# Layer norm of a two-layer decoder trunk: moments summed while tiles are finished, statistics with tokens on partitions, two units prepared for the next stage

## The reference

```python
def layernorm(x, g, b):
    xf = x.astype(F32)
    mu = jnp.mean(xf, -1, keepdims=True)
    var = jnp.mean(jnp.square(xf - mu), -1, keepdims=True)
    return ((xf - mu) * lax.rsqrt(var + LN_EPS) * g + b).astype(x.dtype)

for layer in range(DEPTH):
    ...
        xp = layernorm(ALPHA * xp + mp, ln1_g[layer], ln1_b[layer])
        xp = layernorm(ALPHA * xp + swiglu(xp, ffn_w_gate[layer], ffn_w_up[layer], ffn_w_down[layer]),
                       ln2_g[layer], ln2_b[layer])
```

## Time and profile before

| | us |
|---|---|
| median of three runs | 1865.85 |
| the three runs | 1865.67, 1865.85, 1878.34 |
| the profiled execution, its own time | 1866.61 |
| its span from the first instruction to the last | 1865.0 |
| TensorE busy in it | 1659.9 (89%) |
| VectorE busy in it | 750.9 (40%) |
| ScalarE busy in it | 648.4 (35%) |
| GpSimd busy in it | 241.7 (13%) |

### The profile page before, as it was taken

One profiled execution on the slowest core, in us unless ns is written; L12 is line 12 of the kernel. 1 busy time (PEld: TensorE's weight loads), 2 busy tenths in 40 slices (PEclk: granted clock), 3 DMA queues, 4 the chain that ended last, 5 costly groups with the idle time before them and its releaser, 6 DMA issues. The chain is left out here.

```text
span 1865.0 us, 31270 instructions
## 1 busy us (share of the span) xinstructions
PE 1659.9 (89%) x12319; PEld 1511.7 (81%) x12321; DVE 750.9 (40%) x1433; ACT 648.4 (35%) x1274; POOL 241.7 (13%) x345
## 2 busy tenths in 40 slices
PE   8995297889999899979956899998687999998996
PEld 7994167789999899869945567766587999998994
DVE  4325963443333322265336554443435333332224
ACT  4424262242222211165326554454315222221113
POOL 1002530110000000010042333331021000000000
PEclk9997598889999999989978699999798999999998
DMA  6332102213223233133342121001312233223321
GB/s 158 91 80 55 31 1 70 67 57 90 82 86 90 76 94 93 40 59 88 83 130 58 46 79 57 1 1 42 96 55 63 87 90 90 84 74 96 91 62 48
DMA packets 253288, 132.40 MB, mean 71 GB/s; under 512 B 45142, under 2 KB 252106, under 8 KB 253002
## 3 DMA queue, kind: packets, MB, share of 16 engines
q1 hardware_dynamic: 251402, 127.39, 24.6%
q0 software_dynamic: 1792, 3.76, 0.7%
HBM read 124.81 MB, written 10.43 MB: 73 GB/s over the span
## 5 line engine op out<-in xcount | busy, mean ns | idle before, releaser
L210 PE MATMUL ps<-x_hi,w_hi 128*128 128x272 f32 x2288 | 476.2, 289 | 4.6 <-DVEq L575 4.2
L214 PE MATMUL ps<-x_hi,w_lo 128*128 128x272 f32 x2288 | 474.9, 289 | 0.0
L212 PE MATMUL ps<-x_lo,w_hi 128*128 128x272 f32 x2288 | 473.2, 288 | 0.0
L227 DVE TENSOR_TENSOR w_lo<-w_raw,w_hi 128x1024 fp32r<-128x1024 f32 (+1 forms) x167 | 226.3, 1355 | 491.5 <-ACT w_hi L220 491.5
L220 ACT ACTIVATE w_hi<-w_raw 128x1024 fp32r<-128x1024 f32 (+1 forms) x179 | 199.8, 1116 | 640.6 <-PE ps L214 633.9
L210 PEld LDWEIGHTS ps<-x_hi,w_hi 128*128 128x128 f32 x2288 | 361.0, 189 | 7.0 <-DVEq L575 4.8
L212 PEld LDWEIGHTS ps<-x_lo,w_hi 128*128 128x128 f32 x2288 | 361.0, 189 | 0.0
L214 PEld LDWEIGHTS ps<-x_hi,w_lo 128*128 128x128 f32 x2288 | 358.7, 190 | 0.0
L210 PE MATMUL ps<-h_hi,w_hi 128*128 128x272 f32 x704 | 147.9, 292 | 9.7 <-DVEq L785 9.7
L214 PE MATMUL ps<-h_hi,w_lo 128*128 128x272 f32 x704 | 147.5, 291 | 0.0
L212 PE MATMUL ps<-h_lo,w_hi 128*128 128x272 f32 x704 | 147.1, 291 | 0.0
(11 more groups left out here) (392 smaller groups left out, 2052.7 us busy)
## 6 DMA issues: line engine op xcount, KB each, us to landing
w_raw<-in_ffn_w_gate SPq DMA_DIRECT2D x44, 512.0 KB, 3.8
...
```

What stands on the lines that cost most here:

```text
L210: pe.matmul(out, c.w_hi[:, slot, k, :], x_hi[:, k0 + k, cols], start=first, stop=False)
L212: pe.matmul(out, c.w_hi[:, slot, k, :], x_lo[:, k0 + k, cols], start=False, stop=False)
L214: last = pe.matmul(out, c.w_lo[:, slot, k, :], x_hi[:, k0 + k, cols], start=False, stop=end)
L227: return dve.tensor_tensor(c.w_lo[:, slot, 0:kt, :], c.w_raw[:, slot, 0:kt, :], c.w_hi[:, slot, 0:kt, :].bitcast(F32), ALU.subtract)
```

## The change

Ahead is now used for all four stages that begin with a norm's product, so that the two first units are loaded in the stage before; slot 0 is split there on both engines, slot 1 only lands there and is split during the norm. Class Moments is added to the two stages that end in xT. After the second tile TensorE makes the mean of tile 0 over its own 128 features; ACT copies it to c.shift, and VectorE subtracts this from every tile. ACT squares each finished tile, POOL sums tiles and squares (tiles 1 to 6), and VectorE does the last two sums. TensorE then multiplies x_sum and the sum of squares as stationary operands, 68 tokens at a time, by one column of the matrix "mean": mean and mean square stand in one bank with 68 tokens on partitions and 8 columns. Variance, root and reciprocal are taken in this form, 68x8. The reciprocal goes back to 128x544 by eight products with the unit matrix, in PSUM, and is read from there. VectorE centres and scales tile by tile. pe_first_pair takes both first units tile by tile; slot 1 takes part in the first three tiles and does its other five after slot 0's last. stage_in_proj uses it in a_in as well, where TensorE now waits for both splits. The PSUM banks in stage_out_proj go round in three units in place of four. Two score buffers of each attention take the new arrays' place.

```diff
+SHARED = 3
+
+
+def pe_first_pair(c, pe, start):
...
+            out = c.ps[:, 2 * slot + h, 0:HALF]
+            pe.matmul(out, c.w_hi[:, slot, k, :], c.x_hi[:, k, cols], start=k == 0, stop=False)
+            pe.matmul(out, c.w_hi[:, slot, k, :], c.x_lo[:, k, cols], start=False, stop=False)
+            last = pe.matmul(out, c.w_lo[:, slot, k, :], c.x_hi[:, k, cols], start=False, stop=k == KT - 1)
+        return last
...
     for k in range(KT):
         start.wait_tile(pe, k)
-        for h in range(2):
-            cols = slice(h * HALF, (h + 1) * HALF)
-            out = c.ps[:, h, 0:HALF]
-            pe.matmul(out, c.w_hi[:, 0, k, :], c.x_hi[:, k, cols], start=k == 0, stop=False)
-            pe.matmul(out, c.w_hi[:, 0, k, :], c.x_lo[:, k, cols], start=False, stop=False)
-            last = pe.matmul(out, c.w_lo[:, 0, k, :], c.x_hi[:, k, cols], start=False, stop=k == KT - 1)
-    return last
+        first = products(0, k)
+        if k < SHARED:
+            products(1, k)
+    for k in range(SHARED, KT):
+        second = products(1, k)
+    return first, second
...
+TOK = 68
+CHUNKS = T // TOK
+MEAN, STAT, ROOT = 6, 4, 4
+
+
+class Moments:
...
+    def pe_level(self, pe):
+
+        c = self.c
+        pe.wait_ge(self.added, 1)
+        for h in range(2):
+            last = pe.matmul(c.ps[:, MEAN + h, 0:HALF], c.k("mean"), c.xT[:, 0, h * HALF:(h + 1) * HALF], start=True, stop=True)
+        last.then_inc(self.level, 1)
...
+        act.activation(halves(c.shift[:, :]), c.ps[:, MEAN:MEAN + 2, 0:HALF], ACT.Copy, scale=float(KT)).then_inc(self.shift_set, 1)
...
+        dve.tensor_tensor(c.xT[:, n, :], c.xT[:, n, :], c.shift[:, :], ALU.subtract).then_inc(self.moved, 1)
...
+        dve.scalar_tensor_tensor(c.xT[:, n, :], c.shift[:, :], -1.0 / ALPHA, c.xT[:, n, :], ALU.mult, ALU.add).then_inc(self.moved, 1)
+
+    def dve_after_add(self, dve, n):
+
+        if n == 1:
+            self.dve_move(dve, 0)
+            self.dve_move(dve, 1)
+        if 1 <= n < KT - 1:
+            self.dve_move_early(dve, n + 1)
...
+        act.activation(c.sq_sum[:, :] if n == 0 else self.sq[:, n % 2, :], c.xT[:, n, :], ACT.Square).then_inc(self.squared, 1)
+
+    def act_ready(self, act):
+
+        act.activation(self.ready[:, :], self.c.eps[:, :], ACT.Sqrt)
...
+        eng.tensor_tensor(c.x_sum[:, :], c.xT[:, 0, :] if n == 1 else c.x_sum[:, :], c.xT[:, n, :], ALU.add).then_inc(self.x_summed, 1)
...
+    def pool_sums(self, pool):
+
+        for n in range(1, KT - 1):
+            self.sum_x(pool, n)
+            self.sum_sq(pool, n)
+
+    def dve_last_sums(self, dve):
+
+        self.sum_x(dve, KT - 1)
+        self.sum_sq(dve, KT - 1)
+
+    def pe_tokens(self, pe, x, at):
+
+        c = self.c
+        for i in range(CHUNKS):
+            pe.matmul(c.ps[0:TOK, STAT, at + i:at + i + 1], x[:, i * TOK:(i + 1) * TOK], c.k("mean")[:, 0:1],
+                      start=at + i == 0, stop=at + i == 2 * CHUNKS - 1, skip_group_check=True)
+
+    def pe_moments(self, pe):
+
+        pe.wait_ge(self.x_summed, KT - 1)
+        self.pe_tokens(pe, self.c.x_sum, 0)
+        pe.wait_ge(self.sq_summed, KT - 1)
+        self.pe_tokens(pe, self.c.sq_sum, CHUNKS)
...
+            last = pe.matmul(c.ps[:, MEAN + h, 0:HALF], c.k("mean"), c.x_sum[:, h * HALF:(h + 1) * HALF], start=True, stop=True)
+        last.then_inc(self.mean_set, 1)
+        pe.wait_ge(self.inverted, 1)
+        for i in range(CHUNKS):
+            h, o = i // 4, i % 4 * TOK
+            last = pe.matmul(c.ps[:, ROOT + h, o:o + TOK], self.rstd[:, i:i + 1].broadcast_to([TOK, P]), c.k("ident")[0:TOK, 0:TOK],
+                             start=i % 4 == 0, stop=i % 4 == 3, skip_group_check=True)
+        last.then_inc(self.spread, 1)
 
     def dve(self, dve, split=None):
         c = self.c
-        dve.memset(self.eps[:, :], EPS).then_inc(self.eps_set, 1)
-        dve.wait_ge(self.mean_done, 1)
-        for k in range(KT):
-            dve.tensor_tensor(halves(c.xT[:, k, :]), halves(c.xT[:, k, :]), c.ps[:, 4:6, 0:HALF], ALU.subtract).then_inc(self.centred, 1)
-        if split:
-            split(0)
-            split(1)
+        e2 = c.ps[0:TOK, STAT, CHUNKS:2 * CHUNKS]
+        dve.wait_ge(self.m2_set, 1)
+        dve.tensor_tensor(self.var[:, :], e2, self.m2[:, :], ALU.subtract).then_inc(self.var_set, 1)
+
+        def centre(k):
+            dve.tensor_tensor(halves(c.xT[:, k, :]), halves(c.xT[:, k, :]), c.ps[:, MEAN:MEAN + 2, 0:HALF], ALU.subtract).then_inc(self.centred, 1)
+
+        def scale(k):
+            dve.wait_ge(self.spread, 1)
+            dve.wait_ge(self.centred, k + 1)
+            dve.scalar_tensor_tensor(halves(c.xT[:, k, :]), halves(c.xT[:, k, :]), c.ln_gb[:, self.which, 0, k:k + 1],
+                                     c.ps[:, ROOT:ROOT + 2, 0:HALF], ALU.mult, ALU.mult).then_inc(self.scaled, 1)
+
         dve.wait_ge(self.rooted, 1)
         dve.reciprocal(self.rstd[:, :], self.std[:, :]).then_inc(self.inverted, 1)
-        dve.wait_ge(self.inverted, 1)
-        dve.wait_ge(self.squared, KT)
+        dve.wait_ge(self.mean_set, 1)
+        centre(0)
+        if split:
+            split(1)
+        centre(1)
         for k in range(KT):
-            dve.scalar_tensor_tensor(c.xT[:, k, :], c.xT[:, k, :], c.ln_gb[:, self.which, 0, k:k + 1], self.rstd[:, :],
-                                     ALU.mult, ALU.mult).then_inc(self.scaled, 1)
-            if split and k >= 2 and k % 2 == 0:
-                self.low(dve, k - 2)
-        if split:
-            self.low(dve, KT - 2)
+            scale(k)
+            if k + 2 < KT:
+                centre(k + 2)
+            if split and k % 2 == 0:
+                self.low(dve, k)
...
-        act.wait_ge(self.eps_set, 1)
-        act.activation(self.ready[:, :], self.eps[:, :], ACT.Sqrt)
-        for k in range(KT):
-            act.wait_ge(self.centred, k + 1)
-            if k >= 2:
-                act.wait_ge(self.var_done, k - 1)
-            act.activation(self.sq[:, k % 2, :], c.xT[:, k, :], ACT.Square).then_inc(self.squared, 1)
-            if split and k in (4, 6):
-                split((k - 4) // 2)
-        act.wait_ge(self.var_done, KT)
-        act.activation(halves(self.std[:, :]), c.ps[:, 6:8, 0:HALF], ACT.Sqrt, bias=self.eps[:, :]).then_inc(self.rooted, 1)
+        act.activation(self.m2[:, :], c.ps[0:TOK, STAT, 0:CHUNKS], ACT.Square).then_inc(self.m2_set, 1)
+        act.wait_ge(self.var_set, 1)
+        act.activation(self.std[:, :], self.var[:, :], ACT.Sqrt, bias=c.eps[0:TOK, :]).then_inc(self.rooted, 1)
+        if split:
+            split(1)
...
+                if start.early:
+                    act.sem_inc(hi_made, 1)
                 start.act(act, hi)
...
-                pe.wait_ge(lo_made, 1)
-                pe_first_unit(c, pe, start).then_inc(unit_used, 1)
+                pe.wait_ge(lo_made, 2)
+                for last in pe_first_pair(c, pe, start):
+                    last.then_inc(unit_used, 1)
                 start.pe_late(pe, 6)
-                for n in range(1, len(slabs)):
+                for n in range(2, len(slabs)):
...
+                    sp.wait_ge(hi_made, n - 1)
+                    sp.wait_ge(lo_made, n - 1)
+                    if n < KT:
+                        load_unit(c, sp, n % 2, row_of(w, slice(n * P, (n + 1) * P)), raw_loaded[n % 2])
+                    else:
+                        ahead.load_slot(sp, n - KT)
+                ahead.wait_raw(sp, 1)
...
+                    if n == KT - 1:
+                        act.wait_ge(unit_used, KT - 1)
+                        ahead.split_hi(act, 0)
+                    if n == 1:
+                        moments.act_level(act)
+                        moments.act_square(act, 0)
+                    if n:
+                        moments.act_square(act, n)
+                moments.act_ready(act)
...
+                    if n == KT - 1:
+                        ahead.split_lo(dve, 0)
+                    dve.wait_ge(unit_used, n + 1)
+                    if n >= 2:
+                        dve.wait_ge(moments.moved, n + 1)
+                    dve.scalar_tensor_tensor(halves(c.xT[:, n, :]), halves(c.xT[:, n, :]), ALPHA,
+                                             c.ps[:, PS(n):PS(n) + 2, 0:HALF], ALU.mult, ALU.add).then_inc(added, 1)
+                    moments.dve_after_add(dve, n)
+                moments.dve_last_sums(dve)
...
+                    if n == 1:
+                        moments.pe_level(pe)
+                moments.pe_moments(pe)
```

398 lines of the change are left out of this document (221 added, 177 removed).

## The result

The changed kernel takes 1851.77 us in the median of eight runs (1846.92 to 1858.24), the kernel before 1868.52 (1865.67 to 1878.34): a ratio of .990 with a 95% interval of .9874 to .9926. That is a gain of about 1%, small but clear of the scatter. The profiled run took 1849.88 beside 1866.61, with spans of 1848.2 and 1865.0.

| stretch (us) | before | after | difference | forecast |
|---|---|---|---|---|
| span's start to VectorE's first copy of an input tile | 7.10 | 6.56 | -.5 | |
| to the end of a_in on TensorE | 147.8 | 156.8 | +9.0 | +7.3 |
| attention, to the first add of a_out | 154.2 | 151.6 | -2.7 | |
| first to last add of a_out | 42.1 | 43.0 | +.9 | +1.2 |
| norm 0, to the product that needs the second unit | 42.98 | 34.27 | -8.7 | -9.8 |

A forecast was written before the change was run, and what follows sets the result against it. TensorE, busy 89% of the span, loses time only where it stands still, mainly four norm stretches (153.4 us). Gains of 32.9 less level 4.6, opening 7.3 and clock 2.0 make 19.0, so 1847 us; range 1838 to 1857.

The forecast's parts named there:

- A: Whole kernel: the time comes out as forecast, 1842 to 1852 us; chance .44.
- D: out_proj: added square sums on POOL hold up VectorE's low parts of weights, 4.2 us lost, 1851; chance .08.
- E: up0 and up1: second unit's early end is worthless, gate's next unit waits for silu on ACT; 2 x 2.5 lost, 1852; chance .04.
- First step, 5.1: Each norm, last add to next stage: add, square, sums, sixteen narrow products and barrier take 5.1 us, bounds 4.7 to 7.9.
- Rival F: Norms: narrow products are bound by stationary loads, .43 a pass, 39.6 us in all, 1887; decided at .27 a pass; chance .04.
- Stage start to the first scaled tile, 4.4: Each norm: 68x8 operations, then VectorE's centring and split beside TensorE's mean and spread, 4.4 us, bounds 3.9 to 5.8.
- VectorE's stretch, 19.9: First scaled tile to first unit's last product: VectorE bounds it, 19.9 us, with a scale priced at .64.
- Second unit, 3.8: After the first unit: three tiles' products lie in earlier waits, so 30 remain at .125, 3.8 us.
- Opening, 7.3: a_in: waiting for both splits and the late norm table delay the third slab, 7.3 us lost, bounds 6.9 to 10.
- Level, 4.6: Four stages: two uncovered fp32 products per stage on TensorE, 1.16 at full clock, 4.6 us lost.
- Clock, 2.0: After the opening's idle time and the wait before each norm's last tile: half clock costs 2.0 us, bounds 0 to 9.
- rival C: Norms: half clock at narrow products and before the last tile, some 1.5 per norm, and clock 2 more, 1855; chance .18.

The follow-up runs named there:

- e5: Changed kernel with the reciprocal rounded to the split format and spread by eight single-pass products in place of eight fp32 ones; 1841.53 us.
- e2: Changed kernel with SHARED = 0, so the second unit's 48 products all come after the first unit; 1855.83 us.
- e7: Changed kernel with the norm's statistics of before (reciprocal on 128x544), keeping the new sums, units ahead and pair; 1893.67 us.
- e1: Changed kernel with stage a_in alone back in its old order: first unit, norms' table, second unit; 1842.49 us, ratio .9887.
- e4: Changed kernel without TensorE's two fp32 products per stage for the mean of tile 0, with the shift set to zero; 1850.79 us.
- e6: Changed kernel with unread products added on TensorE, 12 while it waits for the last sum and 16 after the spread; 1850.00 us.
- b2: Changed kernel with e1's opening, silu's table loaded during the norm, even tiles' shifts after the first silu, SHARED = 5 and e5's spread; 1842.86 us, ratio .9869.
- b3: b2 with SHARED = 6, so six more products lie in the wait ahead of the last tile; 1838.21 us, ratio .9845.

## Why the prediction was right

The forecast was 1847 and a net 19.0; the profiled runs differ by 16.7, the medians by 16.8. The mechanism was right; sizes were off, in both directions, and some of that cancels. The time itself decides little: 1851.77 lies at the slow end of A, and D (1851) and E (1852) name it more closely. Only the stretches tell them apart.

- *First step, 5.1*: measured 4.98. Of the range of .05 to .24 for a pass, the value near the short row was right (.07), as long as the clock is up; at half clock a pass takes .12 (1.95/16). Rival F, in which a pass costs more than .27, falls with this.
- *Stage start to the first scaled tile, 4.4*: measured 5.51, and this is the term that was mis-sized. "Both paths come to about 4" holds for TensorE only with a spread near .12 a pass, the low end of the range that it gave: 2.15 + 16 x .12. The spread stands behind the mean on TensorE, and both came at half clock: 2.15 + 3.52, so .22 a pass. The upper bound, 5.8, held. Four times 1.1 is 4.4 of the 4.7 by which the gains fell short. e5 shows it: with the spread shortened, VectorE doesn't wait, and the tile comes .9 earlier.
- *VectorE's stretch, 19.9*: 19.6. A scale has a pitch of .69 (370.70 to 371.39), neither the .64 that was taken from the centres nor dearer than with its factor in SBUF: there three followed each other at (375.74 - 373.65)/3 = .70. So the Trainium skill's larger fixed cost of a PSUM source (VectorE: DVE Perf Modes, The TRN2 errata) doesn't show as lost time here.
- *Second unit, 3.8*: 3.9, and e2 and e7 show the 2.2 that sharing is worth at norms 0 and 1. "Sharing pays nothing" in c_in: 36.43 against 35.6, an excess no larger than the second step's 1.1.
- *Opening, 7.3*: 7.6 up to the third slab, 9.0 by the end of a_in; the rest is the half clock behind the idle time, which the forecast had in the 2.0 for the clock. The chain was the one named, and e1 gives it all back. That 7.6 comes so near is partly luck: 24 of the pair's products ran at the slow pace, not sixteen, a number that no row of before shows (ten ran so there), and the pair took 14.8 in place of 13.7; its start, counted from the first copy, came .6 earlier, and the wait was .2 shorter.
- *Level, 4.6*: .9 in each of the four stages (e4), 3.7 in all. The two products take 1.08 there, not 1.16.
- *Clock, 2.0*: the waits ahead of the last tile did not cost in the profiled run of the changed kernel, but the clock fell there in e6 and, at some 1.1 to 1.5 each, in e1, e5 and b2. The narrow products fell to half clock, as in rival C, at one norm or more of every run with the change but e6 and b3, in whole or in part (in the changed kernel's at norm 3, 1.66 for the second group), at up to 1.5 a norm.
- D and E: the adds of a_out come .9 later in all, which is the level, so POOL's sums delay nothing (D is wrong). E named the right chain on ACT; with SHARED = 3 it isn't yet reached, with 7 it is (2.49).

What the forecast had no term for are the attention stages: -2.7 and about +2.9 in the profiled run. They nearly cancel, by luck. The first goes with the granted clock (.75 in that stretch, .72 before); in the second it reads .90 both times, and no run shows what the 2.9 are.
